# Folding the two halves of gate and up: eight transposes into two PSUM banks and a pair sum on VectorE, in place of sixteen fp32 products

## The reference, cut to what matters

```python
def swiglu(h, w_gate, w_up, w_down):
    return (jax.nn.silu(h @ w_gate) * (h @ w_up)) @ w_down

def moe_swiglu(h, router_w, w_gate, w_up, w_down):
    logits = (h @ router_w).astype(jnp.float32)
    top_val, top_idx = lax.top_k(logits, TOP_K)
    top_w = jax.nn.softmax(top_val, axis=-1)
    gates = jnp.sum(jax.nn.one_hot(top_idx, N_EXPERTS, dtype=jnp.float32) * top_w[..., None], axis=-2)
    y = jnp.zeros_like(h)
    for e in range(N_EXPERTS):
        y = y + gates[..., e:e + 1] * swiglu(h, w_gate[e], w_up[e], w_down[e])
    return y
```

## Time and profile before

| | |
|---|---|
| three runs | 1874.96 us median (1874.5 to 1878.66) |
| the profiled execution | 1874.06 us, span 1872.3 us, mean granted TensorE clock 0.971 |
| PE busy | 1717.6 us, 92% |
| DVE busy | 1373.3 us, 73% |
| ACT busy | 1089.4 us, 58% |
| DMA | 503.87 MB, mean 269 GB/s |

### The profile page before, as it was taken

The page is one execution under the profiler, slowest core; times in us unless marked ns, Lnnn a source line. Parts: engine busy times, 40 slices in busy tenths (PEclk is TensorE's granted clock), DMA queues, the critical chain, the costliest instruction groups (busy, mean ns, idle before and its releaser), DMA issues. The chain is left out here.

```text
span 1872.3 us, 26144 instructions
## 1 busy us (share of the span) xinstructions
PE 1717.6 (92%) x9941; PEld 1390.4 (74%) x9941; DVE 1373.3 (73%) x1236; ACT 1089.4 (58%) x1075; POOL 51.3 (3%) x100
## 2 busy tenths in 40 slices
PE   0998899899999998989898999999999999999996
PEld 0998798679999875666676777767677766788784
DVE  4557456657776669559678887987988688897885
ACT  2334443553333345457766667777767677767673
POOL 2000000001111000000000000000000000000000
PEclk9998999899999999988899999999999999999998
DMA  9975177038887622239888998988999899999992
GB/s 295 306 254 203 57 259 266 5 115 284 307 300 260 226 84 88 83 143 360 313 291 308 342 361 290 391 321 317 363 346 359 300 348 357 378 346 340 366 344 91
DMA packets 244301, 503.87 MB, mean 269 GB/s; under 512 B 10296, under 2 KB 82144, under 8 KB 244192
## 3 DMA queue, kind: packets, MB, share of 16 engines
q1 hardware_dynamic: 228688, 451.44, 67.9%
q0 software_dynamic: 13824, 50.34, 7.4%
q10 hardware_dynamic: 1680, 0.60, 0.2%
HBM read 501.29 MB, written 1.05 MB: 268 GB/s over the span
## 5 line engine op out<-in xcount | busy, mean ns | idle before, releaser
L1353 DVE TENSOR_TENSOR wlo<-raw,whi 128x2048 fp32r<-128x2048 f32 x428 | 968.4, 2286 | 339.2 <-ACT whi L546 338.3
L546 ACT ACTIVATE whi<-raw 128x2048 fp32r<-128x2048 f32 x428 | 807.4, 1910 | 240.6 <-PE ps L855 99.6
L1174 PE MATMUL ps<-whi,ahi 128*128 128x512 f32 x896 | 301.5, 413 | 14.7 <-ACT whi L546 8.5
L1178 PE MATMUL ps<-wlo,ahi 128*64 128x512 f32 (+1 forms) x896 | 262.1, 400 | 16.6 <-DVE wlo L1353 16.6
L851 PE MATMUL ps<-ahi,whi 128*128 128x256 f32 x832 | 237.6, 286 | 5.0 <-issue 3.0
L855 PE MATMUL ps<-alo,whi 128*128 128x256 f32 x832 | 236.5, 284 | 0.0
L858 PE MATMUL ps<-ahi,wlo 128*128 128x256 f32 x832 | 236.5, 284 | 0.0
L1174 PEld LDWEIGHTS ps<-whi,ahi 128*128 128x128 f32 x896 | 168.5, 193 | 61.2 <-issue 24.3
L1178 PEld LDWEIGHTS ps<-wlo,ahi 128*64 128x64 f32 (+1 forms) x896 | 138.5, 157 | 91.2 <-DVE wlo L1353 28.1
L851 PEld LDWEIGHTS ps<-ahi,whi 128*128 128x128 f32 x832 | 160.4, 193 | 6.3 <-issue 6.0
L855 PEld LDWEIGHTS ps<-alo,whi 128*128 128x128 f32 x832 | 160.4, 193 | 0.3
(11 more groups left out here) (235 smaller groups left out, 2044.7 us busy)
## 6 DMA issues: line engine op xcount, KB each, us to landing
raw<-l_exp_w_gate SPq DMA_DIRECT2D x112, 1024.0 KB, 7.3
raw<-l_exp_w_up SPq DMA_DIRECT2D x112, 1024.0 KB, 7.7
raw<-l_exp_w_down SPq DMA_DIRECT2D x112, 1024.0 KB, 6.9
mraw<-mod_w POOLq DMA_DIRECT2D x96, 512.0 KB, 5.9
raw<-l_w_in SPq DMA_DIRECT2D x42, 1024.0 KB, 5.2
raw<-l_ffn_w_gate SPq DMA_DIRECT2D x14, 1024.0 KB, 5.2
raw<-l_ffn_w_up SPq DMA_DIRECT2D x14, 1024.0 KB, 7.2
raw<-l_ffn_w_down SPq DMA_DIRECT2D x14, 1024.0 KB, 6.0
```

Source lines behind the costliest of these rows:

```text
L546: act.activation(whi[s % SPL][:, :], raw[s % RAW][:, :], ACT.Copy).then_inc(hi_done, 1)
L1174: ins = pe.matmul(dst, stat, whi[s % SPL][:, a:a + BANK], start=start, stop=False, skip_group_check=True)
L1178: ins = pe.matmul(dst, stat, wlo[s % SPL][:, a:a + BANK], start=False, stop=stop, skip_group_check=True)
L1353: dve.tensor_tensor(wlo[s % SPL][:, :], raw[s % RAW][:, :], whi[s % SPL][:, :].bitcast(F32), ALU.subtract).then_inc(lo_done, 1)
```

## The change

The two halves are no longer added by the matmul. TensorE transposes `sb_g` into bank 6 and `sb_u` into bank 7 with eight plain transposes against the 128 x 128 identity (`turned_halves`). DVE then sums the pairs (column t and column 64 + t of each chunk) with one `tensor_reduce` over both banks, 1024 elements read and 512 written to `sb_sum` in SBUF. Silu and the multiplication read `sb_sum` instead of PSUM; silu waits for the sum (`gu_sum`). Since bank 6 was used by others, they move or wait: the hidden transposes of the wide block go to bank 4, TensorE waits for the readers of bank 6 in a few steps (`bank6_read`), and a middle now waits for `gu_sum` of its step. The `fold` matrix, its one DVE instruction and its wait go.

```diff
-        fold = arena[:, 13056:13120]
+        sb_sum = arena[:, 1536:2048].rearrange("p (c t) -> p c t", c=8)
...
-            def hidden_high(f):
+            def hidden_high(f, b=6):
                 act.wait_ge(t_done, f + 1 - NHALF)
-                act.activation(hhi[:, :], bank(6), ACT.Copy).then_inc(hhi_done, 1)
+                act.activation(hhi[:, :], bank(b), ACT.Copy).then_inc(hhi_done, 1)
...
                     n = steps_b(*before) + 1
-                    act.wait_ge(tb_done, n)
-                    act.activation(sb_s, bank(7, 0, 4 * HP), ACT.Silu).then_inc(sb_silu, 1)
+                    act.wait_ge(gu_sum, n)
+                    act.activation(sb_s, sb_sum[:, 0:4, :], ACT.Silu).then_inc(sb_silu, 1)
...
-            def folded_T(n):
+            def turned_halves(n):
                 pe.wait_ge(ub_copied, n)
-                waits(pe, hb_done, n - 1)
-                for at, half in ((0, sb_g), (4 * HP, sb_u)):
+                waits(pe, gu_sum, n - 1)
+                for b, half in ((6, sb_g), (7, sb_u)):
                     for fc in range(4):
-                        ins = pe.matmul(bank(7, at + fc * HP, at + fc * HP + HP), half[:, fc * P:fc * P + P], fold,
-                                        start=True, stop=True)
+                        ins = pe.transpose(bank(b, fc * P, fc * P + P), half[:, fc * P:fc * P + P], ident)
                 ins.then_inc(tb_done, 1)
...
+            bank6_read = {(0, 5): (selT_e, 1), (0, 6): (xg_done, gathers(WIDE + 1)), (WIDE + 1, 2): (selT_e, 2),
+                          **{(q, 6): (selT_e, q + 1) for q in range(WIDE + 1, FIRST_M)}}
...
                     pe.wait_ge(gb_copied, steps_b(*before) + 1)
-                    fold_before = lambda: folded_T(steps_b(*before) + 1)
+                    if (q, i) in bank6_read:
+                        pe.wait_ge(*bank6_read[q, i])
+                    fold_before = lambda: turned_halves(steps_b(*before) + 1)
...
                 if middle:
+                    if before is not None and has_b(PASSES[before[0]]):
+                        pe.wait_ge(gu_sum, steps_b(*before) + 1)
                     waits(pe, yb_add, added)
                     middle()
...
-            dve.tensor_tensor(fold, ident[:, 0:HP], ident[:, HP:P], ALU.add).then_inc(fold_done, 1)
...
                     n = steps_b(*before) + 1
+                    dve.wait_ge(tb_done, n)
+                    halves = ps[:, 6 * BANK:8 * BANK].rearrange("p (c a t) -> p c t a", c=8, a=2)
+                    dve.tensor_reduce(sb_sum, halves, AX, ALU.add).then_inc(gu_sum, 1)
                     dve.wait_ge(sb_silu, n)
                     waits(dve, blo_done, n - 1)
-                    dve.tensor_tensor(sb_h.rearrange("p f t -> p (f t)"), sb_s, bank(7, 4 * HP, 8 * HP),
-                                      ALU.mult).then_inc(hb_done, 1)
+                    dve.tensor_tensor(sb_h, sb_s, sb_sum[:, 4:8, :], ALU.mult).then_inc(hb_done, 1)
```

More of the change, by code:

```diff
@@ L233, in build @@
         sb_u = arena[:, 512:1024]
-        sb_s = arena[:, 1024:1280]
+        sb_s = arena[:, 1024:1280].rearrange("p (f t) -> p f t", f=4)
         sb_h = arena[:, 1280:1536].rearrange("p (f t) -> p f t", f=4)
@@ L364, in build @@
         glo_done = sem("glo_done")
-        fold_done = sem("fold_done")
+        gu_sum = sem("gu_sum")
         stored = sem("stored")
@@ L788, in step @@
                 if before is not None and has_a(PASSES[before[0]]):
-                    hidden_high(NHALF + steps_a(before[0]) + before[1] + rr)
+                    hidden_high(NHALF + steps_a(before[0]) + before[1] + rr, 4 if before[0] == WIDE else 6)
                 high(s + 2 + SPL, rr)
@@ L1025, in open_banks, with hidden_T @@
                     pe.matmul(bank(b), zb[:, :], zb[:, :].unsqueeze(1).broadcast_to([P, BANK // P, P]), start=True, stop=False, skip_group_check=True)
-            def hidden_T(f):
+            def hidden_T(f, b=6):
                 pe.wait_ge(h_ready, f + 1)
                 for fc in range(4):
-                    ins = pe.transpose(bank(6, fc * P, fc * P + P), hsb[:, fc * P:fc * P + P], ident)
+                    ins = pe.transpose(bank(b, fc * P, fc * P + P), hsb[:, fc * P:fc * P + P], ident)
                 ins.then_inc(t_done, 1)
@@ L1278, in step @@
                 if before is not None and has_a(PASSES[before[0]]):
-                    hidden_T(NHALF + steps_a(before[0]) + before[1] + rr)
+                    hidden_T(NHALF + steps_a(before[0]) + before[1] + rr, 4 if before[0] == WIDE else 6)
                 if middle:
+                    if before is not None and has_b(PASSES[before[0]]):
+                        pe.wait_ge(gu_sum, steps_b(*before) + 1)
                     waits(pe, yb_add, added)
@@ L1332, in _ @@
             gather(0, 4)
-            pe.wait_ge(fold_done, 1)
             idle_products(1, ((xg_done, 1), (ghi_done, 1)))
@@ L1867, in step @@
                 if before is not None and has_a(PASSES[before[0]]):
-                    hidden_low(NHALF + steps_a(before[0]) + before[1] + rr, bank(6))
+                    hidden_low(NHALF + steps_a(before[0]) + before[1] + rr, bank(4 if before[0] == WIDE else 6))
                 low(s + 2 + SPL, rr)
```

## The result

| | before | after |
|---|---|---|
| median of the runs | 1876.81 us (4 runs, 1874.5 to 1880.36) | 1921.49 us (4 runs, 1918.97 to 1922.17) |
| profiled execution | 1874.06 us, span 1872.3 | 1921.46 us, span 1919.4 |
| granted TensorE clock, mean | 0.971 | 0.966 |

The ratio is 1.0238 (95% interval 1.0224 to 1.0253): 2.4% slower, where 1901 us had been forecast with a range up to 1919.

A forecast was written before the change was run, and what follows sets the result against it. VectorE was taken to pace S steps (+1.6 us per fold), TensorE the L steps (-0.9). Terms over 42 folds summed to +27.3 us on the profiled 1874.06, giving 1901 us, range 1879 to 1919.

The forecast's parts named there:

- the second term of the sum over the 42 folds: Seven steps behind an L step: TensorE already idle, `hlo` comes 1.6 us later each, +11.2 us in all.
- a rival with 5%: TensorE's longer gap behind L steps halves its clock, 5 us in each of 7 steps: 1936 us; chance 5%.
- the sign that it had named for it: Profile windows with PEclk under 1.00 from 1040 to 1500 us would mean the clock fell.
- the first pass: Six folds: three at +1.5, two at the lower clock at -1.6, one at +0.8; +2.1 us in all.
- Which instruction releases the down tiles: Behind an L step the down tiles wait for `hlo`, which DVE makes behind the multiplication and two `low`.
- TensorE's saving: Every fold: eight transposes (0.72 to 0.8 us) replace sixteen records (1.70 us), saving 0.9 us.
- The sum: DVE's new `tensor_reduce` of 1024 elements per fold: 1.2 us, bounds 0.65 and 2.3.
- The round trip: At every fold DVE stands still 0.45 us while silu waits for the sum and the multiplication for silu.
- The pairs' 2.7 us: Runs of two further S steps: 2 x 1.6 less 0.5 idle, 2.7 us each, three times +8.1.
- The scatter of a triple's third step: In the third S step it starts 0.8 us late, hidden under the 1.6 us per fold DVE costs.
- The last steps: The last 7 folds, fourth S pass and on, paced mostly by TensorE: +4.0 us in all.
- two folds at the lower clock: One in the first pass at -1.6 us, one among the last at -1.0, as TensorE's saving.

The follow-up runs named there:

- e1_fill: The changed kernel with idle bf16 products on TensorE in the gaps of the seven steps behind an L step: 1910.73 us, ratio 1.019.
- e3: The kernel before, with one DVE reduce over 1440 constants ahead of the multiplication in the seven steps behind an L step: 1897.44 us, ratio 1.0123.
- e4: The kernel before, with the 1440-constant DVE reduce and idle bf16 TensorE products in the seven steps behind an L step: 1888.54 us, ratio 1.0069.
- e6_later_product: The changed kernel with DVE's multiplication behind the first `low`, `hhb`'s low part behind the second, ACT's copy behind its next `high`: 1915.84 us, ratio 1.0209.
- e7_only_L: The kernel before, with the new transposes and sum in the seven L steps alone, old fold in the other 35: 1872.08 us, ratio 0.9975.
- e2_dummy_all: The kernel before, with one DVE reduce over 1024 constants ahead of the multiplication in all 42 steps: 1904.8 us, ratio 1.0145.
- e5_small_sum: The changed kernel with the pair sum over only 8 of the 64 tokens: 1887.21 us, ratio 1.0045.
- e8_small_sum_fill: The changed kernel with the sum over 8 of 64 tokens and idle products in the seven steps behind an L step: 1877.25 us, ratio 1.001.

## Why the prediction was wrong, and where it was right

The direction and the mechanism held: DVE sets the pace of the S steps, and what it gets it passes on. The size did not.

*The step that failed* is the second term of the sum over the 42 folds, "7 folds in the step behind an L step ... 7 x 1.6 = +11.2". It measures 7 x 3.37 = +23.6, and these 12.4 us are most of the 15.1 by which the steps' sum of 42.4 passes 27.3. The delay in it was right: 23.5 us with the clock kept (e1_fill), 23.4 with the delay put into the old kernel (e3, e4), against 21.8. What was missing is the clock, which the prediction had as a rival with 5%; the sign that it had named for it, PEclk under 1.00 between 1040 and 1500 us, is there. That rival had the place and the sign right and erred twice. It took 5 us for each fall from rows of the first pass and a stretch of 10 us, where it measures 1.55 for a stretch of 3.4 us and 2.2 to 2.6 for one of 6.8. And it made TensorE's gap one of 2.6 us, where there are two, 1.57 and 2.37, or 3.94 in all against 1.56 before. It counted the 0.9 us that the fold saves and left out the delay, and the last up tile's `low` is late as well. At the price that it has, the forecast with the rival taken as certain would have been 1901 + 7 x 1.55 = 1912. The other 9 us to 1921 are the later first fold (2.9), 1.8 behind the last fold, two long stretches (2 x 0.65), 0.7 of delay (1.7 a step for 1.6), and some 2.5 of the smaller misses below.

The Trainium skill, "TensorE: Matmul & The Clock Gate", "Part 4: PE-mode transpose", was the prediction's argument for that rival, and the cause was not there: the clock fell nearly as often with sixteen plain products in the fold (six of seven steps in e3_dummy_behind_L), and the four transposes that stand in these steps in every kernel brought no fall before. The section "A second HAM failure mode: psum-queue depth-cycling" of the same page fits the rows better; it says of a bf16 kernel that TensorE, idle briefly and often between groups of products, made the clock swing. The trace agrees in this: two gaps of 1.57 and 2.37 us, with 1.1 us of products between, and half clock behind them.

*Which instruction releases the down tiles.* The prediction named `hlo`. The profile names ACT's copy of the up bank, L793, before and after, and by the ends it is right: L793 ends at 1258.67 + 0.60 = 1259.27, `hlo` at 1258.42 + 0.68 = 1259.10, and the product starts at 1259.52. The number didn't suffer, since the kernel waits for both there, and both stand behind the multiplication, each on its engine, and are moved alike. No run here separates them.

*What held.* TensorE's saving is 0.91 us per fold, forecast 0.9 (transposes 0.79 for eight). The sum is 1.216 us, forecast 1.2. The round trip leaves DVE idle 0.48 us, forecast 0.45. The pairs' 2.7 us are what was forecast. In that number two small things cancel: the rows give 1253.33 - 1251.63 = 1.70 us a fold from the sum's start to the multiplication's, not 1.6, because the sum is followed by idle time and nothing overlaps its end. That is also the 1.7 us of delay behind an L step. By it a pair would cost 2 x 1.70 - 0.5 = 2.9, and it measures 2.7; the difference was not taken apart. The scatter of a triple's third step starts 0.9 us later behind its fold, forecast 0.8:

```profile
1386.03 1.04 PE L1206 MATMUL ps<-cst,arena 128*128 128x128 f32 x8
...
1390.58 1.98 PE L1246 MATMUL ps<-arena 128*128 128x512 f32 x4 [1.67 <-DVE arena L1863]
```

Before it was 1359.05 - 1355.41 = 3.64 us; it is 4.55. As forecast, it costs a triple nothing beyond DVE's own time.

*Smaller misses.* The last steps cost 5.4 us in place of 4.0, and the first pass 3.2 in place of 2.1. Most of it lies at two folds at the lower clock, which had been priced as TensorE's saving alone, -1.6 and -1.0. The step from 846.15 us went from 17.72 to 17.08 us (-0.6) and the one from 1579.62 from 16.37 to 15.99 (-0.4), while DVE's idle time in them fell from 3.0 to 0.7 and from 1.7 to 0.5 us. That fits DVE setting their pace after the change; no run shows it. The remaining 0.9 us stay open.

## What to carry to other kernels

Ask of each place which engine paces it, and put a trade between two engines only where the one that gains is the one that paces: the same edit is worth -0.9 us in an L step, +0.9 to +1.7 in a step of a pair or triple and +2.8 to +3.9 in the step behind an L step, and used in the seven L steps alone it beats both kernels. Where a change lengthens a standstill of TensorE, price the clock besides the delay, with the pitch of products at the lower clock and not with a stretch from another part of the kernel; and look at every gap near it, not at the longest alone. A producer that moves into another engine's list adds its wait to both lists: moving the consumer back on one of them (e6_later_product) shifts the idle time to the other.

## What the runs showed of the hardware beyond that

- A `tensor_reduce` over pairs that lie 64 columns apart in two PSUM banks, 1024 elements read, takes 1.216 us. One over 1024 neighbouring constants in SBUF takes 1.21 us, and a `tensor_tensor` of 1024 elements 1.218: neither the stride nor PSUM made it longer.
- From the end of the sum on DVE to the start of silu on ACT and back to the multiplication, DVE is idle 0.48 us in all 18 folds between 1040 and 1400 us where it waits.
- In the steps behind an L step the granted clock fell the more often, the longer TensorE stood still ahead of the low products of the last up tile and of the down tiles together. It fell in none of seven behind one gap of 1.56 us (before, and the same in e7_only_L), and in four of seven behind one of 2.37 (e2_dummy_all). Behind two gaps it fell in six of seven at 0.51 and 2.38 us (e3_dummy_behind_L), and in seven of seven at 0.64 and 2.37 (e5_small_sum), 1.57 and 2.37 (the changed kernel) and 0.67 and 3.10 (e6_later_product). It fell in none where idle bf16 products left 1.29 and 0.91 us (e1_fill).
- Idle products cost TensorE nothing where it was waiting anyhow (11.18 against 11.17 us above), but the falls they prevent can turn up elsewhere: three in the pairs' second step in e1_fill, none there in e4_dummy_behind_L_fill or e8_small_sum_fill.
